# A decoder layer with 32 experts on one core: one down-weight load cut into twelve loads of eight partitions and one of thirty-two

## The reference, cut to what matters

```python
def _moe(x2d, w_router, b_router, w_gate_up, b_gate_up, w_down, b_down):
    logits = x2d.astype(jnp.float32) @ w_router.astype(jnp.float32) + b_router.astype(jnp.float32)
    top_v, top_i = lax.top_k(logits, TOP_K)
    gates = jax.nn.softmax(top_v, axis=-1)
    ...
    def expert_block(args):
        xb, e = args
        h = xb @ w_gate_up[e] + b_gate_up[e]
        return _clamped_swiglu(h) @ w_down[e] + b_down[e]
```

## Time and profile before

| | us |
|---|---|
| device time, median of 3 runs | 1120.46 (1119.97 to 1120.77) |
| span of the profiled execution | 1110.5 |
| PE busy | 990.5 (89%) |
| DVE busy | 392.3 (35%) |
| data queue q1, share of 16 DMA engines | 90.8% |
| HBM read | 419.86 MB, 380 GB/s over the span |

### The profile page before, as it was taken

The page is one execution under the profiler, slowest core; times in us unless marked ns, Lnnn a source line. Parts: engine busy times, 40 slices in busy tenths (PEclk is TensorE's granted clock), DMA queues, the critical chain, the costliest instruction groups (busy, mean ns, idle before and its releaser), DMA issues.

```text
span 1110.5 us, 16610 instructions
## 1 busy us (share of the span) xinstructions
PE 990.5 (89%) x6600; PEld 422.0 (38%) x6600; DVE 392.3 (35%) x896; ACT 205.7 (19%) x446; POOL 13.5 (1%) x11
## 2 busy tenths in 40 slices
PE   6999999999998999889998999789789879979967
PEld 5777764333333333222332233233233223323323
DVE  7987545231322132223222133123333323222222
ACT  4875332111111111111101011011111111101101
POOL 3000000000000000000000000000000000000000
PEclk9989999999999999989999999899999999989999
DMA  9414953999999999999999999999999999999996
GB/s 364 129 54 138 421 233 148 379 425 427 411 427 426 427 426 428 426 427 427 417 427 427 427 426 428 428 426 428 425 430 428 426 426 428 429 426 427 428 422 246
DMA packets 43132, 425.22 MB, mean 383 GB/s; under 512 B 11412, under 2 KB 14612, under 8 KB 16560
## 3 DMA queue, kind: packets, MB, share of 16 engines
q1 hardware_dynamic: 41280, 421.82, 90.8%
q10 hardware_dynamic: 1728, 2.11, 0.6%
q0 software_dynamic: 48, 0.15, 0.0%
HBM read 419.86 MB, written 2.51 MB: 380 GB/s over the span
## 4 chain that ended last, share of the span: by engine, by line
PE 54%; DMA 37%; DVE 4%; ACT 2%; issue 2%; ACTq 1%; SPq 0%; DVEq 0%
PE banks L543 52%; DMA gu_ring<-w_gu_dram 37%; PE banks L933 1%; DVE raw L1942 1%; ACT x_tok L1367 1%; PE banks L889 0%; DVE hl L1954 0%; DVE hT L1959 0%; PE banks L679 0%; PE banks L1017 0%; PE banks L940 0%; ACT gath L1378 0%; PE banks L1010 0%; ACT raw_s L1422 0%; ACT pT L1290 0%
## 5 line engine op out<-in xcount | busy, mean ns | idle before, releaser
L1988 DVE TENSOR_TENSOR xT<-xT,banks 128x576 f32<-128x576 f32 x128 | 91.1, 751 | 537.2 <-PE banks L543 537.1
L543 PE MATMUL banks<-gu_ring,xe 128*64 128x512 f32 x1152 | 266.3, 599 | 13.7 <-DMA gu_ring<-w_gu_dram 13.3
L543 PE MATMUL banks<-gu_ring,xe_s 128*32 128x512 f32 x1152 | 156.7, 645 | 44.7 <-DMA gu_ring<-w_gu_dram 36.5
L543 PEld LDWEIGHTS banks<-gu_ring,xe 128*64 128x64 f32 x1152 | 75.3, 136 | 167.2 <-issue 139.1
L543 PE MATMUL banks<-dn_ring,hT 128*64 128x512 f32 x576 | 129.3, 597 | 4.9 <-DVE hT L1959 4.9
L543 PEld LDWEIGHTS banks<-gu_ring,xe_s 128*32 128x32 f32 x1152 | 29.0, 112 | 132.0 <-issue 79.3
L543 PE MATMUL banks<-dn_ring,hT_s 128*32 128x256 f32 x1152 | 67.8, 381 | 3.2 <-ACT xe_s L1412 3.2
L543 PEld LDWEIGHTS banks<-dn_ring,hT 128*64 128x64 f32 x576 | 39.2, 137 | 79.4 <-issue 73.0
L1393 ACT ACTIVATE raw<-banks 128x512 f32<-128x512 f32 x18 | 10.7, 597 | 232.9 <-PE banks L543 232.9
L543 PE MATMUL banks<-x_tok,oh 96*64 96x512 f32 x216 | 50.3, 601 | 0.0
L543 PE MATMUL banks<-gT,ye 64*128 64x288 f32 x288 | 49.2, 465 | 0.0
(11 more groups left out here) (350 smaller groups left out, 862.0 us busy)
## 6 DMA issues: line engine op xcount, KB each, us to landing
gu_ring<-w_gu_dram SPq DMA_DIRECT2D x120, 2048.0 KB, 24.4
dn_ring<-w_dn_dram SPq DMA_DIRECT2D x63, 2048.0 KB, 21.7
gu_ring<-w_gu_dram SPq DMA_DIRECT2D x16, 1024.0 KB, 8.6
w_out<-w_out_dram SPq DMA_DIRECT2D x2, 2048.0 KB, 9.9
w_in<-w_in_dram SPq DMA_DIRECT2D x3, 1024.0 KB, 16.1
w_in<-w_in_dram SPq DMA_DIRECT2D x4, 512.0 KB, 10.3
w_glu<-w_glu_dram SPq DMA_DIRECT2D x1, 2048.0 KB, 8.9
dn_ring<-w_dn_dram SPq DMA_DIRECT2D x2, 1024.0 KB, 22.0
```

The costliest lines, as they stand in the source:

```text
L543: return nc.tensor.matmul(out, lhsT, rhs, start=start, stop=stop, **kw)
L1988: X.tensor_tensor(two, two, pair[(1, 3)[n % 2]].rearrange("p (h f) -> p h f", h=2)[:, :, 0:T], ALU.add).then_inc(S("acc_done"), 1)
```

## The change

The second down slot of position 30, `dn_ring[1]`, is loaded differently. Before, it was the second transfer of `dn(x[0], NE - 4, 0)`. Now the call is written out: the wait for the slot and the load of the first slot are as before, and the second slot's 128 rows are loaded by twelve transfers of 8 partitions (rows 0 to 95), which count on a semaphore of their own, `dn_spread`, and one of 32 partitions (rows 96 to 127), which counts on `dn_in[1]`. PE waits for all twelve, beside the wait for `dn_in[1]`, ahead of part 2 of position 30's down product.

```diff
+SPREAD = 12
...
-    S("tail_done"), S("dn_last")
+    S("tail_done"), S("dn_last"), S("dn_spread")
...
-        dn(x[0], NE - 4, 0)
+        for h in range(2):
+            sp.wait_ge(S("dn_used"), (NE - 4) * 4 + 2 * (h + 1))
+            if h == 0:
+                load_dn(sp, x[0], 0, 0)
+        src = a["w_dn"][bass.ds(x[0], 1), 2:4].rearrange("o c p k f -> (o c p k) f").rearrange("(p i) f -> p i f", i=4)
+        for b in range(SPREAD):
+            rows = slice(8 * b, 8 * b + 8)
+            sp.dma_start(dn_ring[1][rows], src[rows]).then_inc(S("dn_spread"), 16)
+        sp.dma_start(dn_ring[1][8 * SPREAD:], src[8 * SPREAD:]).then_inc(dn_in[1], 16)
...
-        def down(w, s, kind, after, s_after, j, fill):
+        def down(w, s, kind, after, s_after, j, fill, spread=False):
...
                 if kind == "few" and c % 2 == 0:
                     pe.wait_ge(dn_in[2 * j + c // 2], fill * 16)
+                if spread and c == 2:
+                    pe.wait_ge(S("dn_spread"), SPREAD * 16)
...
-        expert(NE - 2, N_WIDE, N_SLIM - 2, "few", "mid", "few", 0, PAIRS)
+        expert(NE - 2, N_WIDE, N_SLIM - 2, "few", "mid", "few", 0, PAIRS, spread=True)
```

More of the change, by code:

```diff
@@ L1062, in gate_bias, with expert @@
                     last.then_inc(S("comb_done"), 1)
-        def expert(p, w, s, kind, before, after, j, fill):
+        def expert(p, w, s, kind, before, after, j, fill, spread=False):
             w_before, s_before = w - (before != "few"), s - (before != "mid")
@@ L1103, in expert @@
                 residual(LAST_PARTS[2])
-            down(w, s, kind, after, s_after, j, fill)
+            down(w, s, kind, after, s_after, j, fill, spread)
         gather(0)
```

## The result

The changed kernel takes 1137.1 us (median of 4, 1131.58 to 1139.43) against 1120.38 us (median of 4, one execution more than in the table before): a ratio of 1.0155, 95% interval 1.012 to 1.0189. It is 16.7 us slower. Forecast were 1127.0 us and a range of 1117.8 to 1137.0; the time lies 0.1 us above the range and the loss is 2.6 times the forecast one. Run again beside three experiments, the same kernel came to 1135.95 us against 1119.65 (1.0155, interval 1.0105 to 1.0204).

A forecast was written before the change was run, and what follows sets the result against it. The weight stream was taken to bound the kernel, its late eight engines setting each landing. Narrow rows cost +12.6 us less a 6.2 us lead, +6.4, with issues and wait at 0: 1120.46 + 6.4 = about 1127 us, range 1117.8 to 1137.0.

The forecast's parts named there:

- What bounds the kernel: From 300 us on the weight stream at about 427 GB/s sets the pace; landings x us later end it x later.
- SP's issues and PE's wait at nothing: At position 30's slot, twelve more issues (6.2 to 7.8 us) are covered and PE's added wait is met: 0.
- Crowding at the target: Narrow transfers write few partitions per engine, so their rows land slower than 0.614 us each; taken as 2.1 times.
- The factor of 2.1: Slowdown per row in the 8-partition transfers, the middle between one halving step (1.6) and two (2.6).
- the factor 1.6: Slowdown for one halving of partitions per engine, from two small copies (0.55 / 0.34 us); used for the 32-row transfer.
- Crowding confined to the eight engines that carry the narrow rows: Only the half carrying the narrow rows slows, working 17.5 us in place of 4.9: +12.6 us.
- its lead of 6.2 us: Eight engines finish the stream about 6.2 us early; if they carry the narrow rows, +12.6 shrinks to +6.4 us.
- The narrow rows on one half as a whole: Each 8-partition transfer runs on the same eight engines, all of one half, early or late.
- The rival of the late half: Narrow rows fall on the late engines: +3.7 us without crowding (1124.1, chance 0.07), +12.6 with it (1133.1, chance 0.13).
- the stretch at 0.50: End of the stream with only eight engines working; expected again, or grown from 6.5 to some 14 us for the late half.
- the first rival: No crowding, narrow rows on the early half: worked as -2.5 us, taken as -2.0, 1118.5 us; chance 0.27.
- theory D: From the experiments: all engines run at half rate from the first engine's entry into a cut transfer until the last leaves.

The follow-up runs named there:

- e8: Changed kernel with the slot as one 128-partition load, its twelve narrow transfers cut to 32 bytes per partition into a spare tile: ratio 1.0011, issue to end +0.7 us.
- e1: Changed kernel, but each of the twelve transfers takes every fourth partition at source and target: ratio 1.0101 to the kernel before, issue to end +12.3 us.
- e2: Changed kernel, but the twelve transfers read every fourth row at the source only: ratio 1.0100 to the kernel before, issue to end +20.1 us.
- e3: Changed kernel, but the twelve transfers write every fourth partition at the target only: ratio 1.0097 to the kernel before, issue to end +11.6 us.
- r1: The changed kernel itself run again, six executions: ratio 1.0155 to the kernel before, issue to end +17.5 us.
- r2: Changed kernel with every fourth partition at source and target, run again, six executions: ratio 1.0123 to the kernel before, issue to end +11.2 us.
- r3: Changed kernel with every fourth row at the source only, run again, six executions: ratio 1.0171 to the kernel before, issue to end +17.8 us.
- e5: Changed kernel, but the slot is loaded by two transfers, of 96 and 32 partitions: ratio 1.0141 to the kernel before, issue to end +11.7 us.
- e10: Kernel before, with position 2's second down slot cut into 96 and 32 partitions, position 30 as before: ratio 1.0038, issue to end +4.2 us.
- e4: Changed kernel, but the slot is loaded by six transfers of 16 partitions and one of 32: ratio 1.0124 to the kernel before, issue to end +16.6 us.
- e7: Changed kernel, but the slot is loaded by four transfers of 32 partitions: ratio 1.0149 to the kernel before, issue to end +12.6 us.
- e11: Changed kernel with the slot as one 128-partition load, after six eight-row copies from HBM to HBM: ratio 1.0017 to the kernel before, issue to end +2.0 us.
- e9: Changed kernel, but three quarters of the slot's columns load whole, the last quarter as 96 and 32 partitions: ratio 1.0047, issue to end +4.6 us.
- e12: Changed kernel, but the whole slot is loaded by sixteen transfers of 8 partitions: ratio 1.0163 to the kernel before, issue to end +19.0 us.

## Why the prediction was wrong, point by point

- *What bounds the kernel.* Right: the end moves with the landings. Of the 18.7 us, 17.9 are there when position 30's last slot lands.
- *SP's issues and PE's wait at nothing.* Right: +0.7 us with both and without the bulk (e8).
- *Crowding at the target.* Right in kind: share 1.0, GB/s down to 197, large packets of 1.22 us in place of 0.614, and of source and target the target alone matters (e1 to e3, r1 to r3). Its size had no such ground. The factor of 2.1 was for a row in a narrow transfer and grew with each halving of the partitions per engine; the measured 2.0 is the mean over all packets, and it is as large where an engine writes 6 and 2 partitions (e5). With the factor 1.6 for both, the same working gives that cut (8 x 0.614 x 1.6) - 4.9 = +3.0 us before any lead; it cost 11.7. That 2.1 and 2.0 agree is luck.
- *Crowding confined to the eight engines that carry the narrow rows.* This is the step that failed: "The half that carries them then works 12 x 0.614 x 2.1 = 15.5 us ... 17.5 against 4.9, +12.6 us." In fact all sixteen slow down, those on regular loads too. The stream as a whole lost 13.4 us.
- *"If it is the early half, it first uses up its lead of 6.2 us".* This failed with it. The lead was there (5.6 us by the landings, 1065.7 against 1071.3). If every engine is slowed there is no one to catch up with, so nothing may be subtracted. Most likely the lead even lengthens the stretch: 4.2 us for a cut among level engines, 11.7 us among engines 6 to 7 us apart (e10, e5). Without the subtraction the working would have read +12.6, against 13.4 measured for that term; as the two come about differently, that they are near each other is luck too.
- *The narrow rows on one half as a whole.* Eight engines carry them, as forecast, but six are of the early half and two of the late one (e8). So the lead could never have paid for all of them: by the prediction's own rule, that the last engine sets every landing, two late carriers are enough for the late half's +12.6. The rival of the late half was the nearer one, at 1133.1. The last two engines kept position 30's fourth slot open for 4.7 us, about what is left of the loss, 17.9 - 13.4 = 4.5 us (in r1 three engines ended late, 3.2 to 6.7 us behind the rest). That the 6 rows more on two late engines, 3.7 us at the full rate, are what holds them back was argued, not tested alone; from 1075 to 1090 us the stream, at 397, 390 and 377 GB/s, also misses another 1.4 us.
- *Not in the sum:* 0.9 us of PE at a lower clock after it had stood idle.

- *What the profile would show.* A share near 1.0 at a low GB/s and longer packets came as described. The halves afterwards did not: the stretch at 0.50 neither came back nor grew to 14 us, it went.
- *A slip in the range.* Its lower end was put at the first rival's -2.7, where that rival's own working gives -2.5. It changes nothing here.

Together 13.4 + 4.5 + 0.9 = 18.8 us, against 18.7 from issue to end and 16.7 between the medians. The 4.5 is a remainder, so this sum is no check; what is measured on its own is the 13.4, the 4.7 and the 0.9.

The Trainium skill's "SBUF — State Buffer", section "Door 1: The DMA port swizzle", gave 28.9 us for the twelve narrow transfers and an end 20 us later; the trace has a slow stretch of about 30 us and an end 18.7 us later. The agreement in size should not be taken for its mechanism: by it a packet of a narrow transfer would take 2.4 us, and a cut into 96 and 32 should cost at most about that much (an estimate by that page: the 32 rows reach eight ports, four rows of 16.4 KB each at 27.2 GB/s are 2.4 us, if nothing overlaps), while large packets take 1.22 us on average and that cut costs 11.7 us.

What stays open: why a cut into 96 and 32 partitions, with every engine at its 8 rows, already halves the rate of all sixteen. The runs show that it comes with bulk writes into SBUF by transfers of fewer than 128 partitions (e4, e5, e7), not with twelve such transfers of 32 bytes a row (e8) nor with copies within HBM (e11). Which engine writes which partition no view tells. That engines then stand in one another's way at the same partitions would fit, but was argued, not shown, and for the cut into 96 and 32 source and target were not told apart. e9, e10 and e12 miss the simple rule of theory D by 1 to 3.5 us each.

## What to carry to other kernels

Where weight loads of full height keep all DMA engines busy, don't cut a load by partitions: one slot of 2 MB cut so cost 11 to 20 us of a 1120 us kernel late in the stream, however few pieces there were, and 4 us early in it. If it has to be cut, columns are the thing to try: the kernel's own last slot is loaded in two halves by columns, and there eight engines at a share of 0.50 still move 213 GB/s. No run cut position 30's slot by columns alone. When a cut slows a shared stream, look at GB/s beside the DMA share: with packets of the same size, a full share at half the rate means that each packet takes twice as long, and the missing bytes divided by the full rate give the loss of the stream as a whole; a few engines that end late come on top. A lead of some engines over others is not a reserve: before subtracting it, ask whether the added cost falls only on those that have it.

## What the runs showed of the hardware that was not expected

- A 2 MB load of 96 + 32 partitions among loads of 128 held the whole stream at 210 to 234 GB/s for some 20 us (427 otherwise), with all engines busy.
- Four transfers of 8 neighbouring partitions beside one of 96 cost as much (+17.8 us) as twelve (+17.5 to +18.7).
- Six copies of eight 16 KB rows within HBM ran on sixteen engines, in packets of 8 KB, and left the stream at 423 to 433 GB/s (e11).
- A transfer of eight partitions ran on eight engines, six of the early half and two of the late one (e8). At 1060 us into the kernel the two halves were some 6 us apart, at 213 us all sixteen engines within 1 us.
- A load of eight neighbouring partitions took SP 0.45 us per issue (12 in 5.42 us), one of every fourth partition 0.84 (12 in 10.09 us, e1).
- Executions of one unchanged kernel differed by up to 14 us (1111.8 to 1126.0), with the mean clock of the span between 0.966 and 0.979 in them.
